# Odd input projection of a hybrid decoder trunk: VectorE's order inside a step (convolution taps and values, then the weight's low half, then the long taps)

## The chip, the cores and the metric

The kernel runs on one core of a Trainium2 chip. The metric is the device time of one execution in microseconds (us), median over runs; less is better. Engines are named as in the profile: PE is TensorE's matmul and PEld its weight load, DVE is VectorE, ACT is ScalarE, POOL is GpSimd, SP is the engine that issues most DMAs.

## The reference, cut to what matters

Two decoder layers over 512 tokens of width 1024. The change lies in layer 1 (the odd one), in its combined input projection and what is done to that projection's output while it is still being computed:

```python
p = h @ od_w_in[j]                       # 1024 -> 3600 columns
y_c = _conformer_conv(p[..., :o1], ...)  # val * sigmoid(gate), causal depthwise conv of 31 taps, LN, silu
y_d = _mamba2_ssd(p[..., o1:o2], p[..., o2:o3], p[..., o3:], ...)
# in _mamba2_ssd:
xbc = jax.nn.silu(_causal_dwconv(xbc, conv_w, conv_b))     # 4 taps over 1536 channels
dt = jax.nn.softplus(dt_raw + dt_bias)
xdt = x_c * dt_c[..., None]                                # the "values", per chunk of 128 tokens
states = jnp.einsum('bclgn,bclgh,bclghp->bcghpn', b_c, decay_to_end, xdt)
```

## The kernel before

All weights come as one stream of 512 KB chunks (128 x 1024 fp32), three slots deep (`W_SLOTS`). A product in fp32 accuracy is made of three fp32r products (`mm3`, lines 615 to 617), so each weight chunk is split first: ACT writes the high half (`w_hi`, line 1289), DVE subtracts it from the raw weights and writes the low half (`w_lo`, line 1822, `split`, which raises `w_split`). PE waits for `w_split` before a chunk. A chunk of the feature-major projection is 8 blocks of three 128x512 matmuls, 24 in all, into one of the 8 PSUM banks.

The odd input projection has 29 chunks: 0 to 7 are gates and values of the Conformer branch, 8 is dt, 9 to 20 are xbc 0 to 11, 21 to 28 are z. One loop of 29 steps on DVE and one on ACT run beside PE's 29 chunks, each engine in the written order. In step i:

- DVE splits chunk i+2 (`split(FIRST["in1"] + i + W_SLOTS)`), then does the 3 remaining taps of the short convolution of xbc i-10, which is chunk i-1 (`ssd_conv(i - 10)`, steps 10 to 21; it reads the PSUM bank, adds into `sconv`, and its third tap raises `xbc_out`), then some taps of the long convolution (`conf_taps`: 2 in each of steps 10 to 21, 4 in steps 22 and 23), then at a few steps small pieces (`conf_sum`, dt work in steps 9, 15, 16, 18), and in steps 20 to 23 the two multiplications `values(i - 20)` that empty the banks `sxt` into `xdt`.
- ACT makes `w_hi` of chunk i+2 (not before PE is through chunk i-1, whose slot it takes), waits for chunk i of PE, copies it with the first tap into `sconv` (`ssd_first(i - 9)`), makes three products for the long convolution (`conf_product`, tile `cprod`; the third waits for POOL's addition of the first), and applies the gate to the convolution of step i (`ssd_gate(i - 10)`, which waits for `xbc_out`).
- POOL adds the three products (line 584, `cacc2 <- cacc2 + cprod`), both operands in SBUF.
- PE computes chunk i. Between chunks it has inserted work: dt transposes before 15, `slast` before 18, `values_to_tokens(c)` (8 transposes into two `sxt` banks) before 20 + c, keys and scores before 24, chunk states before 25, and so on.

Banks go round in a fixed order worked out at build time (`TILES`, `BANK`, `AFTER`; `take` waits until the earlier tile of that bank is emptied). For the chunks that the prediction speaks of: chunk 15 takes the bank of xbc 3 (emptied in DVE's step 13), chunk 16 that of xbc 4 (step 14), chunk 17 that of xbc 5 (step 15), chunk 19 xbc 6 (step 16), chunk 20 xbc 8 (step 18), the `sxt` pair before 21 one of xbc 9 (step 19), chunk 21 xbc 10 (step 20), chunk 22 xbc 11 (step 21), chunk 23 the second `sxt` bank of `values(1)` (step 21), and chunk 24 the first `sxt` bank of `values(3)` (step 23). Chunk c also needs its low half, from step c-2.

Of the kernel before, what the change touches and what calls it, by code (L numbers as in the profile page):

```python
# [28 lines left out]
W_SLOTS = 3  # L29
# [35 lines left out]
FIRST = {}  # L65
# [105 lines left out]
def build(nc, x_tok, x_feat, mem_feat, weights, vectors, lora, lru_w, ln_rows, out):  # L171
    with ExitStack() as ctx:
# [177 lines left out]
        def xdt(c):  # L350

            return xdts[c // 2][:, c % 2]
# [13 lines left out]
        def S(name):  # L366
            if name not in sems:
                sems[name] = ctx.enter_context(nc.semaphore(name))
            return sems[name]

        def V(name, i):
            c = VEC[name] + i
            return vec[:, c:c + 1]

        def bank(stg, i):
            return ps[BANK[stg, i]]
# [6 lines left out]
        def made(kind, n):  # L383

            return S("mixer_mm"), MADE[kind][n - 1]
# [7 lines left out]
        def bc(ap, n):  # L393

            return ap.unsqueeze(2).to_broadcast([ap.shape[0], ap.shape[1], n])
# [1397 lines left out]
        def _(dve):  # L1793
# [3 lines left out]
            def step(ins, lag=0):  # L1797

                n_step[0] += 1
                ins.then_inc(S("dve_step"), 1)  # L1800
                if n_step[0] > lag:
                    dve.wait_ge(S("dve_step"), n_step[0] - lag)
# [3 lines left out]
            def done(ins, name):  # L1806

                counts[name] = counts.get(name, 0) + 1
                ins.then_inc(S(name), 1)
                dve.wait_ge(S(name), counts[name])  # L1810

            def f(ap):

                return ap.bitcast(F32)

            def split(upto):

                while n_split[0] < min(upto, N_CHUNKS):
                    c = n_split[0]
                    s = c % W_SLOTS  # L1820
                    dve.wait_ge(S("w_hi_done"), c + 1)
                    dve.tensor_tensor(w_lo[:, s], w_raw[:, s], f(w_hi[:, s]), ALU.subtract).then_inc(S("w_split"), 1)  # L1822
                    n_split[0] += 1
# [10 lines left out]
            def tt(o, a, b_, op):  # L1834
                return dve.tensor_tensor(o, a, b_, op)  # L1835

            def stt(o, a, s, b_, op0, op1):
                return dve.scalar_tensor_tensor(out=o, in0=a, scalar=s, in1=b_, op0=op0, op1=op1)  # L1838
# [277 lines left out]
            def scale_rows(n, t):  # L2116

                l, which = divmod(n, 3)
                dve.wait_ge(*of(f"lnt{l}_{which}", "_mm", 8))
                dve.wait_ge(S("gb_in"), 16 * (n + 1))  # L2120
                step(tt(h[:, t], h[:, t], gb[:, 0], MUL))

            def shift_rows(n, t):

                done(tt(h[:, t], h[:, t], gb[:, 1], ADD), "h_ready")
# [204 lines left out]
            def conf_taps(first, last):  # L2330

                for n in range(first, last):
                    j, k = divmod(n, DVE_TAPS)
                    k += POOL_TAPS + 1
                    at = CP - (CONF_TAPS - 1) + k
                    acc = bank("cacc", j)[:]
                    dve.wait_ge(S("c_first"), j + 1)
                    step(stt(acc, cu[:, j, at:at + T], V("ccw", 4 * k + j), acc, MUL, ADD))

            def conf_sum(j):  # L2340

                dve.wait_ge(S("c_add"), (POOL_TAPS - 1) * (j + 1))
                done(tt(cacc[:, j], bank("cacc", j)[:], cacc2[:, j % 2], ADD), "cacc_out")

            def ssd_conv(m):

                x_, d_ = bank("xbc", m), sconv[:, m % 2]
                dve.wait_ge(S("s_first"), m + 1)
                for k in range(1, 4):
                    ins = stt(d_[:, k:T], x_[:, 0:T - k], V("scw", 12 * (3 - k) + m), d_[:, k:T], MUL, ADD)  # L2350
                    if k < 3:
                        step(ins)
                    else:
                        done(ins, "xbc_out")

            def taps_by(i):

                at = [0, 0, 0, 3, 8, 13, 18, 23, 28, 31]
                return at[i] if i < 10 else min(31 + 2 * (i - 9) if i < 22 else 55 + 4 * (i - 21), 4 * DVE_TAPS)

            def by_head(ap):
                return ap.rearrange("p (h v) -> p h v", v=64)

            def values(c):

                for q in range(2):
                    dve.wait_ge(*made("sxt", 2 * c + q + 1))
                    done(tt(by_head(xdt(c)[:, q * HALF:q * HALF + HALF]), by_head(bank("sxt", 2 * c + q)[:]),
                            bc(stm[:, 0, c, 8 * q:8 * q + 8], 64), MUL), "sxt_out")

            def next_state(c):

                for g in range(2):
                    dve.wait_ge(*out_sem("sst", 2 * c - 2 + g + 1))
                    cols = slice(g * HALF, g * HALF + HALF)
                    nxt = by_head(prev[:, c, cols])
                    step(tt(nxt, by_head(prev[:, c - 1, cols]), bc(stm[:, 3, c, 8 * g:8 * g + 8], 64), MUL))
                    dve.wait_ge(*made("sst", 2 * c + g + 1))
                    done(tt(nxt, nxt, by_head(bank("sst", 2 * c + g)[:]), ADD), "sst_out")

            def grown(c):

                dve.wait_ge(S("h_moved"), 32)
                for g in range(2):
                    dve.wait_ge(*made("yoff", 2 * c - 2 + g + 1))
                    done(tt(by_head(yoff[:, c - 1, g * HALF:g * HALF + HALF]), by_head(bank("yoff", 2 * c - 2 + g)[:]),
                            bc(done_of(GROWTH, c)[:, 8 * g:8 * g + 8], 64), MUL), "yoff_out")
# [1 line left out]
            counts["sst_out"] = 2  # L2389
            step(dve.memset(cu[:, :, 0:CP], 0.0))  # L2390
            for i in range(29):
                split(FIRST["in1"] + i + W_SLOTS)
                if i < 4:
                    scale_rows(2, i)
                    shift_rows(2, i)
                if 2 <= i < 10 and i % 2 == 0:
                    j = i // 2 - 1
                    dve.wait_ge(S("cgate_out"), j + 1)
                    dve.wait_ge(S("chunk_done"), FIRST["in1"] + i)
                    done(tt(cu[:, j, CP:CP + T], bank("cval", j)[:], p1[:, 4 + j, PAD:PW], MUL), "cval_out")  # L2400
                if 10 <= i < 22:
                    ssd_conv(i - 10)
                if i:
                    conf_taps(taps_by(i - 1), taps_by(i))
                if i in (10, 14, 20, 24):
                    conf_sum((10, 14, 20, 24).index(i))
                if i == 9:

                    dve.wait_ge(S("s_sums"), 1)
                    dve.wait_ge(S("masks"), 2)  # L2410
                    raw = p1[0:16, DT, PAD:PW]
                    step(stt(sdt[:, 0], raw, 0.0, sdt[:, 0], ALU.max, ADD))
                    step(dve.tensor_scalar(raw, sdt[:, 0], small[0:16, 200:201], -1.0, MUL, MUL))
                    done(dve.tensor_tensor_scan(sdt[:, 1], m_scan[0:16], raw, 0.0, MUL, ADD), "s_acum")
                if i == 15:
                    for m in range(2):
                        dve.wait_ge(*made("stok", m + 1))
                        done(dve.tensor_copy(stm[:, m].rearrange("p c h -> p (c h)"), bank("stok", m)[:, 0:64]),
                             "stok_out")
                if i == 16:  # L2420
                    dve.wait_ge(S("masks"), 4)
                    dve.wait_ge(S("s_sums"), 2)
                    done(tt(to_sums[32:48], sdt[:, 1], f(sums_hi[:]), SUB), "s_alo")
                if i == 18:

                    dve.wait_ge(S("slast_out"), 1)
                    done(tt(stm[:, 2], stm[:, 3], stm[:, 1], SUB), "s_dte")
                if 20 <= i < 24:
                    values(i - 20)
                if i == 26:  # L2430
                    dve.wait_ge(*made("c", 1))
                    for j in range(4):
                        ins = stt(cacc[:, j], bank("cmean", 0)[:], -1.0 / 512, cacc[:, j], MUL, ADD)
                        done(ins, "c_cent")
                    done(dve.tensor_copy(small[:, 255:256], small[:, 254:255]), "cmean_out")
                    next_state(1)
                    grown(1)
                if i == 27:
                    next_state(2)
                if i == 28:  # L2440
                    grown(2)
# [163 lines left out]
```

## Time and profile before

| | us |
|---|---|
| median of 3 runs | 1705.49 |
| lowest and highest of the three | 1677.04, 1707.43 |
| the profiled execution | 1680.34 |
| its span | 1678.6 |

PE is busy 97% of the span, DVE 59%, ACT 44%, POOL 10%. The odd input projection takes the stretch from about 831 to 1031 us. A matmul's row is about 0.39 us long, but starts follow each other by 0.227 us (0.427 us at the half clock), since matmuls are pipelined: a chunk of 24 takes 5.44 us. In the rows below "idle before" in square brackets is the time for which the engine had nothing to do ahead of that instruction, and the arrow names who ended it. An xN at the end of a row means that N instructions were merged, in one duration.

### The profile page before, as it was taken

How to read it: one execution, taken by the hardware profiler on the slowest of the kernel's cores; microseconds unless marked ns; L12 is line 12 of the kernel's file. 1: busy time of each engine (PE TensorE's matmuls, PEld its weight loads, DVE VectorE, ACT ScalarE, POOL GpSimd, SP SyncE). 2: the span in 40 equal slices, each digit the busy share in tenths (PEclk: the TensorE clock that was granted, in tenths of full speed). 3: DMA queues.
4: the chain of work that ended last, by engine and by line, in shares of the span. 5: the costliest groups of instructions: out<-in, count | busy, mean ns of one | idle time of the engine just before them, and what ended most of it. 6: DMA issues, size and time to landing. Idle time of an engine off the chain costs nothing.

```text
span 1678.6 us, 24671 instructions
## 1 busy us (share of the span) xinstructions
PE 1620.1 (97%) x9954; PEld 1348.3 (80%) x9954; DVE 991.9 (59%) x1236; ACT 738.4 (44%) x987; POOL 168.9 (10%) x175
## 2 busy tenths in 40 slices
PE   7999999999999999999998899999999999999997
PEld 5777887988878888888786777879888788888886
DVE  3569767755676443434698955656656654444345
ACT  4545644555253232323457745634552532323232
POOL 5101201002000000000045620000020000000001
PEclk9999999999999999999999999999999999999999
DMA  5222004442223332334242220234411333323331
GB/s 201 68 88 64 16 4 151 140 149 63 84 81 101 100 101 88 101 96 130 63 149 78 88 73 4 101 128 149 139 64 56 108 102 100 100 89 102 99 125 63
DMA packets 41297, 159.60 MB, mean 95 GB/s; under 512 B 4576, under 2 KB 4704, under 8 KB 39776
## 3 DMA queue, kind: packets, MB, share of 16 engines
q1 hardware_dynamic: 40896, 155.93, 29.0%
q10 hardware_dynamic: 288, 2.10, 0.3%
q8 instruction: 79, 1.29, 0.3%
q14 instruction: 34, 0.28, 0.1%
HBM read 153.81 MB, written 4.19 MB: 94 GB/s over the span
## 4 chain that ended last, share of the span: by engine, by line
PE 83%; DVE 10%; ACT 4%; issue 1%; POOL 1%; DMA 0%; SPq 0%; DVEq 0%; ACTq 0%; POOLq 0%
PE bank L615 25%; PE bank L616 25%; PE bank L617 25%; DVE mix L1835 1%; DVE act_lo L1835 1%; DVE w_lo L1822 1%; PE bank L817 1%; PE bank L802 1%; DVE sconv L1838 1%; DVE h L1838 1%; DVE bank L1838 1%; PE bank L1138 1%; ACT w_hi L1289 1%; PE bank L1010 0%; DMA w_raw<-weights 0%
## 5 line engine op out<-in xcount | busy, mean ns | idle before, releaser
L1822 DVE TENSOR_TENSOR w_lo<-w_raw,w_hi 128x1024 fp32r<-128x1024 f32 x263 | 325.8, 1240 | 299.0 <-ACT w_hi L1289 295.9
L615 PE MATMUL bank<-act_lo,w_hi 128*128 128x512 f32 x1048 | 416.7, 398 | 28.8 <-DVE w_lo L1822 16.0
L1289 ACT ACTIVATE w_hi<-w_raw 128x1024 fp32r<-128x1024 f32 x263 | 278.9, 1061 | 348.9 <-PE bank L617 338.5
L616 PE MATMUL bank<-act_hi,w_lo 128*128 128x512 f32 x1048 | 411.4, 393 | 0.0
L617 PE MATMUL bank<-act_hi,w_hi 128*128 128x512 f32 x1048 | 411.0, 392 | 0.0
L615 PEld LDWEIGHTS bank<-act_lo,w_hi 128*128 128x128 f32 x1048 | 198.8, 190 | 78.3 <-issue 17.1
L617 PEld LDWEIGHTS bank<-act_hi,w_hi 128*128 128x128 f32 x1048 | 198.9, 190 | 42.2
L616 PEld LDWEIGHTS bank<-act_hi,w_lo 128*128 128x128 f32 x1048 | 198.8, 190 | 41.3 <-issue 1.2
L615 PE MATMUL bank<-w_lo,aux_hi 128*128 128x512 f32 x576 | 224.7, 390 | 0.0
L617 PE MATMUL bank<-w_hi,aux_hi 128*128 128x512 f32 x576 | 224.2, 389 | 0.0
L616 PE MATMUL bank<-w_hi,aux_lo 128*128 128x512 f32 x576 | 224.1, 389 | 0.0
L615 PEld LDWEIGHTS bank<-w_lo,aux_hi 128*128 128x128 f32 x576 | 108.1, 188 | 23.1 <-DVE w_lo L1822 0.7
L617 PEld LDWEIGHTS bank<-w_hi,aux_hi 128*128 128x128 f32 x576 | 108.1, 188 | 22.7
L616 PEld LDWEIGHTS bank<-w_hi,aux_lo 128*128 128x128 f32 x576 | 108.1, 188 | 22.0
L584 POOL TENSOR_TENSOR cacc<-cacc,cprod 128x512 f32<-128x512 f32 x52 | 71.9, 1382 | 484.7 <-ACT cprod L1631 482.2
L615 PE MATMUL bank<-w_lo,act_hi 128*128 128x512 f32 x288 | 113.5, 394 | 2.8 <-DVE w_lo L1822 2.3
L617 PE MATMUL bank<-w_hi,act_hi 128*128 128x512 f32 x288 | 112.9, 392 | 0.0
L616 PE MATMUL bank<-w_hi,act_lo 128*128 128x512 f32 x288 | 112.7, 391 | 0.0
L1835 DVE TENSOR_TENSOR stage<-stage 128x512 f32<-128x512 f32 x64 | 44.3, 692 | 105.7 <-ACT stage L1599 105.7
L1599 ACT ACTIVATE stage<-bank 128x512 f32<-128x512 f32 x64 | 38.2, 597 | 143.7 <-PE bank L617 143.7
L1835 DVE TENSOR_TENSOR aux_lo<-stage,aux_hi 128x512 fp32r<-128x512 f32 (+1 forms) x66 | 48.9, 741 | 61.7 <-ACT aux_hi L1601 53.6
L1601 ACT ACTIVATE aux_hi<-stage 128x512 fp32r<-128x512 f32 x64 | 40.5, 632 | 59.8 <-DVE stage L1835 59.8
(330 smaller groups left out, 1978.1 us busy)
## 6 DMA issues: line engine op xcount, KB each, us to landing
w_raw<-weights SPq DMA_DIRECT2D x263, 512.0 KB, 3.5
gb<-ln_rows SPq DMA_DIRECT2D x6, 1024.0 KB, 5.9
stage<-x_feat SPq DMA_DIRECT2D x4, 512.0 KB, 6.0
h<-x_tok SPq DMA_DIRECT2D x1, 2048.0 KB, 7.3
stage<-mem_feat ACTq DMA_DIRECT2D x2, 1024.0 KB, 6.4
spill<-h SPq DMA_DIRECT2D x1, 2048.0 KB, 6.9
h<-spill SPq DMA_DIRECT2D x1, 2048.0 KB, 7.9
out<-h SPq DMA_DIRECT2D x3, 512.0 KB, 2.6
```

The costliest lines, as they stand in the source:

```text
L584: pool.tensor_tensor(cacc2[:, j % 2], cacc2[:, j % 2], cprod[:, added % 2], ALU.add)\
L615: pe.matmul(o, whi, xlo, start=first, stop=False)
L616: pe.matmul(o, wlo, xhi, start=False, stop=False)
L617: return pe.matmul(o, whi, xhi, start=False, stop=last)
L802: last = each(lambda c, q, tok, feat, cf, ct: pe.matmul(compact(o, j, c, q, n), M_[b][tok, j, ct], halves(NBH[b][tok, j, ct], n, True), st ...
L817: last = each(lambda c, q, tok, feat, cf, ct: pe.matmul(compact(o, j, c, q, n), left[tok, j, ct], halves(right[tok, j, ct], n, v < 5), sta ...
L1289: act.activation(w_hi[:, s], w_raw[:, s], ACT.Copy).then_inc(S("w_hi_done"), 1)
L1599: done(act.activation(stage[:, n % 2], bank(f"up{l}_{q}", i)[:], ACT.Relu), "up_out")
L1601: done(act.activation(aux_hi[:, i], stage[:, 2 + n % 2], ACT.Copy), "up_hi")
L1822: dve.tensor_tensor(w_lo[:, s], w_raw[:, s], f(w_hi[:, s]), ALU.subtract).then_inc(S("w_split"), 1)
L1835: return dve.tensor_tensor(o, a, b_, op)
L1838: return dve.scalar_tensor_tensor(out=o, in0=a, scalar=s, in1=b_, op0=op0, op1=op1)
```

## The change

In steps 10 to 28 the split of chunk i+2 is moved behind the short convolution, and in steps 20 to 23 `values(i - 20)` is moved from behind the long taps and `conf_sum` to ahead of the split. Steps 0 to 9 are as they were. No instruction is added or removed, on any engine; no wait is added or removed. ACT's, PE's, POOL's and SP's programs are untouched.

```diff
             for i in range(29):
-                split(FIRST["in1"] + i + W_SLOTS)
+                if i < 10:
+                    split(FIRST["in1"] + i + W_SLOTS)
                 if i < 4:
                     scale_rows(2, i)
                     shift_rows(2, i)
...
                 if 10 <= i < 22:
                     ssd_conv(i - 10)
+                if 20 <= i < 24:
+                    values(i - 20)
+                if i >= 10:
+                    split(FIRST["in1"] + i + W_SLOTS)
                 if i:
                     conf_taps(taps_by(i - 1), taps_by(i))
...
-                if 20 <= i < 24:
-                    values(i - 20)
```

## Rows read from the trace of the kernel before

**Rows 1.** The page: busy time, share of the span and instructions of two engines.
```profile
PE 1620.1 (97%) x9954; PEld 1348.3 (80%) x9954; DVE 991.9 (59%) x1236; ACT 738.4 (44%) x987; POOL 168.9 (10%) x175
```

**Rows 2.** Who waited for whom, 884 to 1035 us: total us, times, longest us.
```profile
DVE w_lo L1822 <- ACT w_hi L1289: 35.8, 15, 8.4
POOL cacc L584 <- ACT cprod L1631: 38.1, 14, 7.7
...
PE bank L615 <- DVE sconv L1838: 5.7, 3, 4.0
PE bank L615 <- DVE w_lo L1822: 3.9, 2, 2.6
...
PE bank L615 <- DVE xdt L1835: 2.0, 1, 2.0
```

**Rows 3.** Timeline of PE: start us, us, engine, line, operation, names, [idle before <- releaser].
```profile
901.30 0.52 PE L615 MATMUL bank<-act_lo,w_hi 128*128 128x512 f32 x1 [2.56 <-DVE w_lo L1822]
...
921.57 0.50 PE L615 MATMUL bank<-act_lo,w_hi 128*128 128x512 f32 x1 [1.19 <-DVE sconv L1838]
933.24 0.50 PE L615 MATMUL bank<-act_lo,w_hi 128*128 128x512 f32 x1 [0.44 <-DVE sconv L1838]
961.40 0.80 PE L615 MATMUL bank<-act_lo,w_hi 128*128 128x512 f32 x1 [4.03 <-DVE sconv L1838]
...
969.35 0.93 PE L1059 MATMUL bank<-ident,p 128*128 128x128 f32 x7
...
975.70 1.03 PE L1059 MATMUL bank<-ident,p 128*128 128x128 f32 x8
...
986.86 0.78 PE L615 MATMUL bank<-act_lo,w_hi 128*128 128x512 f32 x1 [2.01 <-DVE xdt L1835]
994.04 1.88 PE L1088 MATMUL bank<-xdtd,bt 128*128 128x512 f32 x4
```

**Rows 4.** Busy time in four stretches: PE, PEld, DVE, ACT, POOL, granted clock, DMA, GB/s.
```profile
901.00:921.00 20.00, 19.07 (x80) 15.06 (x80) 17.17 (x23) 14.90 (x20) 11.49 (x11) 0.91 0.30 84
921.00:961.00 40.00, 35.36 (x162) 28.84 (x162) 36.93 (x48) 32.93 (x45) 26.02 (x21) 0.98 0.31 93
961.00:987.00 26.00, 23.58 (x113) 19.71 (x113) 20.81 (x28) 15.61 (x22) 7.94 (x6) 0.89 0.25 77
987.00:1033.00 46.00, 46.00 (x185) 33.27 (x185) 19.51 (x26) 16.51 (x23) 5.07 (x4) 0.96 0.11 35
```

**Rows 5.** Timeline of DVE: steps 10, 11, 15, 20, 22 and 23.
```profile
899.05 2.11 DVE L1822 TENSOR_TENSOR w_lo<-w_raw,w_hi 128x1024 fp32r<-128x1024 f32 x1
901.08 2.30 DVE L1838 SCALAR_TENSOR_TENSOR sconv<-bank,vec,sconv 128x511 f32<-128x511 f32 x3
...
906.58 1.23 DVE L1822 TENSOR_TENSOR w_lo<-w_raw,w_hi 128x1024 fp32r<-128x1024 f32 x1 [0.89 <-ACT w_hi L1289]
...
929.74 1.23 DVE L1822 TENSOR_TENSOR w_lo<-w_raw,w_hi 128x1024 fp32r<-128x1024 f32 x1 [0.50 <-ACT w_hi L1289]
930.88 2.31 DVE L1838 SCALAR_TENSOR_TENSOR sconv<-bank,vec,sconv 128x511 f32<-128x511 f32 x3
...
957.90 1.23 DVE L1822 TENSOR_TENSOR w_lo<-w_raw,w_hi 128x1024 fp32r<-128x1024 f32 x1 [0.34 <-ACT w_hi L1289]
959.04 2.31 DVE L1838 SCALAR_TENSOR_TENSOR sconv<-bank,vec,sconv 128x511 f32<-128x511 f32 x3
961.38 1.55 DVE L1838 SCALAR_TENSOR_TENSOR bank<-cu,vec,bank 128x512 f32<-128x512 f32 x2
...
977.87 1.42 DVE L1835 TENSOR_TENSOR xdt<-bank,stm 128x512 f32<-128x512 f32 x2
981.82 1.22 DVE L1822 TENSOR_TENSOR w_lo<-w_raw,w_hi 128x1024 fp32r<-128x1024 f32 x1 [2.53 <-ACT w_hi L1289]
982.96 3.12 DVE L1838 SCALAR_TENSOR_TENSOR bank<-cu,vec,bank 128x512 f32<-128x512 f32 x4
```

**Rows 6.** Timeline of ACT: its wait in iteration 10; high halves of chunks 20 to 22.
```profile
903.46 1.28 ACT L1662 ACT_TABLE_LOAD   x1 [2.57 <-DVE sconv L1838]
...
945.74 1.06 ACT L1289 ACTIVATE w_hi<-w_raw 128x1024 fp32r<-128x1024 f32 x1
...
951.17 1.07 ACT L1289 ACTIVATE w_hi<-w_raw 128x1024 fp32r<-128x1024 f32 x1
952.14 0.76 ACT L1645 ACTIVATE sconv<-bank,vec 128x512 f32<-128x512 f32 x1
...
956.74 1.06 ACT L1289 ACTIVATE w_hi<-w_raw 128x1024 fp32r<-128x1024 f32 x1
```

**Rows 7.** Timeline of POOL: additions beside a split, and later without one.
```profile
876.24 3.54 POOL L584 TENSOR_TENSOR cacc<-cacc,cprod 128x512 f32<-128x512 f32 x2 [0.37 <-ACT cprod L1631]
...
897.90 5.74 POOL L584 TENSOR_TENSOR cacc<-cacc,cprod 128x512 f32<-128x512 f32 x3 [0.41 <-ACT cprod L1631]
...
943.22 2.67 POOL L584 TENSOR_TENSOR cacc<-cacc,cprod 128x512 f32<-128x512 f32 x2 [2.53 <-ACT cprod L1631]
...
953.80 4.04 POOL L584 TENSOR_TENSOR cacc<-cacc,cprod 128x512 f32<-128x512 f32 x3 [1.40 <-ACT cprod L1631]
```

**Rows 8.** Timeline of DVE: the split that ran beside the first of Rows 7.
```profile
876.57 2.05 DVE L1822 TENSOR_TENSOR w_lo<-w_raw,w_hi 128x1024 fp32r<-128x1024 f32 x1
```

## Prediction, made before the change was run

> **What bounds the kernel now.** I read the page first. PE is busy 97% of the span [rows 1], so time can only be won where PE stands still or runs at the half clock. The change touches one loop, so the second view was who waited for whom in that loop. PE waits there for three writers on DVE: 5.7 us for the short convolution (sconv), 3.9 us for the split (w_lo) and 2.0 us for the values (xdt) [rows 2]. DVE itself waited 35.8 us for ACT's high half in the same stretch: it stands ahead of a split that isn't there yet, with other work behind it that could run.
>
> The third view, PE's timeline, gives each stop its place [rows 3]. By counting 5.44 us a chunk (24 x 0.227 us): 901.30 is the start of chunk 12, 921.57 of 15, 933.24 of 17, 961.40 of 21 and 986.86 of 24. The stops cost more than their idle time. Chunk 21 takes from 961.40 to 969.35, 7.95 us instead of 5.44, chunk 24 from 986.86 to 994.04, 7.18 us, and the granted clock is 0.91 and 0.89 in the two stretches that hold a long stop [rows 4]: after it the matmuls run for a while at 1.2 GHz instead of 2.4. So the stop ahead of 21 costs 4.03 + 2.5 = 6.5 us, that ahead of 24 2.01 + 1.7 = 3.7 us, those ahead of 15 and 17 1.2 and about 0.5 us without a slow stretch. About 12 us in all: that is the most the change can win back, since chunk 12's stop (2.56 us and some 1.7 at the half clock) is ended by a split that the change puts later.
>
> The pace of the others: ACT goes round in 951.17 - 945.74 = 5.43 and 956.74 - 951.17 = 5.57 us [rows 6], as long as a chunk. A full step of DVE is split 1.15 + convolution 2.34 + two taps 1.58 = 5.07 us from start to start [rows 5]. DVE has thus 0.4 us of slack per step and pieces of 0.5 to 0.9 us in six of the steps on top.
>
> **The change, part by part.** Nothing is added: DVE does the same 36 convolution taps, splits and values. Only order moves, and with it three things. Behind the moved split stand taps alone, and the convolutions now run in the time in which DVE waited for w_hi.
>
> *Step 10, a loss.* The split of chunk 12 ran at 899.05, and PE stood waiting for it [rows 3, 5]. Its w_hi was ready long before, so there is no wait to fill. Now the convolution's 2.30 us [rows 5] come first: it runs 899.05 to 901.4, the split from 901.4. Before it took 2.11 us, 0.88 more than the usual 1.23, because POOL was adding; POOL's three additions last until 903.6 [rows 7], so the split meets them again in part: it ends between 902.5 and 903.4 instead of 901.16. Chunk 12 starts 1.4 to 2.2 us later, and its longer stop may cost 0 to 0.8 us more at the half clock (by the difference between chunk 21's 2.5 and chunk 12's 1.7). I take +2.5.
>
> *Steps 13 and 15, a gain.* Chunk 15 waited for the convolution of step 13, 17 for that of step 15. In step 15 DVE stood 0.50 us for w_hi, split 1.15 us, and only then convolved [rows 5]. But PE needs the split of the same step as well (chunk 17 = 15 + 2), so it waits for the second of the two whichever is first. Only DVE's idle time is won, 0.34 to 1.06 us in seven of the steps 11 to 20 (0.89 in step 11, the first [rows 5]). The gate of ACT follows the convolution, so ACT comes to its next w_hi sooner: in iteration 10 it stood 2.57 us, until 903.46 [rows 6], for a convolution that now ends at 901.4. The delay of chunk 12 itself also gives DVE and ACT 2 us in which to catch up. With both, neither stop is left: -1.7 us.
>
> *Step 20, a gain.* Chunk 21 takes the bank of xbc 10, which is convolved in step 20, a chunk's time ahead and no more. Before, DVE ended step 19 at 957.56, waited 0.34, split 1.14, convolved until 961.35 [rows 5]. The split there is for chunk 22, which nobody needs yet. Moved behind, it gives 1.5 us at once: 959.9. What DVE has caught up by then comes on top. I chained the durations above from step 10 on, each start at the later of the engine's own last end and what it waits for, PE at 5.44 us a chunk with its insertions as before. With no split lengthened DVE's steps 11 to 20 start at 904.8, 909.9, 915.0, 920.0, 925.8, 931.4, 937.4, 942.4, 948.0 and 953.1 (5.07 us each, the small pieces, and 0.6 us of waits), and chunks 12, 15, 17 and 20 at 902.7, 922.4, 933.3 and 950.5. The convolution of step 20 ends at 955.4, before PE comes at 956.9: no stop at all, chunk 21 starts 4.5 us earlier and loses its slow stretch of 2.5.
>
> *Steps 20 to 23, a gain.* Values(3) came behind a wait of 2.53 us for w_hi, a split and four taps, at 986.1 [rows 5], though their transposes were through at 976.7 [rows 3]. Values(2) ended at 979.29; now values(3) come straight behind step 22, near 980 at the latest. PE is ready for chunk 24 at 986.86 - 2.01 = 984.85. The stop goes wholly: -3.7 us, in every case that I can make. The splits behind them have a whole chunk to spare (that of step 23 is for chunk 25).
>
> *Steps 24 to 28.* The split goes behind nothing new, as there is neither convolution nor values: 0.
>
> *What the moved splits meet, a loss.* A split reads two tensors in SBUF, as POOL's additions do. Where they overlapped, at 876.57, the split took 2.05 us instead of 1.23 [rows 8], and POOL's two additions 3.54 instead of 2.67 [rows 7]: 0.8 us lost on each side. In steps 11 to 20 of before no split met an addition, since each waited for w_hi, which ACT writes just as POOL's third addition ends. The convolution of 2.3 us put ahead pushes the split into the next round of additions unless DVE is early enough to wait for w_hi as before. It isn't in steps 10 to 13, by the chain. So at least four splits pay. If all pay 0.8 us, a step is 5.9 us against PE's 5.44, DVE never gets early, and the same chain gives stops of 0.4 to 0.8 us ahead of chunks 17, 18 and 19 and one of 3.5 us ahead of 21: step 20 starts at 960.5, and chunk 21 at 962.9.
>
> The Trainium skill (SBUF — State Buffer, on the port pair that VectorE and GpSimd share) says that a VectorE operation with two SBUF inputs and a GpSimd one lock each other out for a whole instruction, and the loser waits. By that rule one meeting would cost the split what is left of an addition, up to 1.3 us, and the sum would lie between the cases below; the rows at 876 us agree with it, 0.8 us for an addition that had begun 0.33 us earlier.
>
> **The sum**, taken where the stream of chunks stands at 21 (what was lost at 12 and won at 15 and 17 is in its start) and at 24. With no meeting: chunk 21 starts at 956.9 instead of 961.4, -4.5; its slow stretch goes, -2.5; chunk 24's stop goes, -3.7: -10.7 us. With 0.8 us in every step: +1.5 (962.9), 0, -3.7: -2 us. With half of that in every step, which for step 20 is the same as the first five paying in full and the others nothing: the chain puts chunk 21 at 960.0, -1.4, behind a stop of 2.7 us that leaves a slow stretch like chunk 12's (1.7 instead of 2.5), -0.8, and -3.7: -6 us. I take this, since the first four or five splits meet additions and later ones need not. Behind chunk 24 PE has no stop until 1037 and DVE is busy 19.51 of 46.00 us [rows 4], so all of it lasts to the end: every transfer, split and ACT step there follows PE.
>
> The profiled execution took 1680.34 us, 1.7 more than its span. It lies 25 us below the median 1705.49, near the lowest run; the runs spread over 30.4 us, five times what I forecast. Against the profiled time the sum gives 1674.3; applied to the median, 1699.5.
>
> **Rivals.**
> - *No meeting with POOL* (DVE early enough from step 12 on). For it: the splits of 11 to 20 of before met none, and the convolutions of the new order leave DVE waiting for w_hi again once it has caught up. Against: steps 10 to 13. -10.7 us: 1694.8.
> - *Every split meets POOL.* For it: 26.02 us of POOL work in 40.00 us [rows 4], so two thirds of all moments. -2 us: 1703.5.
> - *Slower.* One mechanism: the meetings also hold up POOL, whose first addition releases ACT's third product. ACT's round is 5.44 us with no slack. If each meeting costs ACT 0.8 us too, w_hi comes ever later, the split waits for it and chunks 13 to 20 wait for the split: (5.44 + 0.8 - 5.44) x 8 = 6.4 us, plus chunk 12's 2.5, less the 3.7 us of chunk 24: +5 us, 1710.5. It decides from about 0.2 us a round (0.2 x 8 + 2.5 is over 3.7). Against: only a meeting with the first of the three additions holds ACT, and the splits that come late meet the second or third.
> - *No change at all*: PE waits for both split and convolution, and each stop only changes its name. True for 15 and 17, not for 21 and 24, where the split is for a later chunk. 0 us: 1705.5.
>
> **How the numbers follow.** Forecast (-4 to -8): 0.45. No meeting (-8 to -11): 0.2. Every split meets (-3 to -1): 0.2. No change: 0.05. Slower by 1 to 6: 0.1. All five lie within 2% (34 us), which is about what a measurement of this kernel can tell from no change. The range must hold the spread of the runs too: the low end is the lowest run with the largest gain that still carries weight, 1677 - 9 = 1668; the high end the highest run, 1707, as the losing cases are as likely as a gain on it. A drawn median at the low end would pass -2% (1671.4) only with a gain over 5.6 us: 0.04; slower by over 2%: 0.01; within: 0.95.
>
> **What would show it.** PE's stop ahead of chunk 24 gone, xdt written before PE is through chunk 23. The stop ahead of chunk 12 longer, 4 to 5 us. The stop ahead of chunk 21 below 3 us. DVE's waits for w_hi in 899 to 960 us shorter and now between sconv and w_lo. w_lo rows over 1.8 us, at least three, in steps 10 to 14, with POOL rows over 4.4 us for three additions. It is wrong if the stop ahead of 21 stays at 4 us, if new stops on w_lo stand ahead of chunks 13 to 20, or if a stop appears behind chunk 24.

## The result, and the profile after

| | before | changed |
|---|---|---|
| median, us (runs) | 1680.45 (7) | 1669.14 (7) |
| lowest and highest | 1676.78, 1707.43 | 1667.53, 1702.36 |
| ratio of the times, 95% interval | | 0.9943 (0.9927 to 0.9959) |

The ratio is a gain of 9.6 us, between 6.9 and 12.3 (1680.45 times one less the ratio). Some executions of every kernel here are 24 to 33 us longer than the rest, two of the three of before that were shown at first among them (so its median moved from 1705.49 to 1680.45 with four more runs), and the ratios in this document leave them out.

The profile of the changed kernel that is read here, "the change" from now on, was taken when the same kernel was run a second time: an execution of 1669.68 us with a span of 1668.0, so that its times can be laid beside those of before.

PE's timeline in it, the rows that answer to [rows 3]:

```profile
892.61 0.47 PE L615 MATMUL bank<-act_lo,w_hi 128*128 128x512 f32 x1 [1.38 <-DVE w_lo L1822]
...
902.36 0.77 PE L615 MATMUL bank<-act_lo,w_hi 128*128 128x512 f32 x1 [4.06 <-DVE w_lo L1822]
...
921.52 0.67 PE L1043 MATMUL bank<-ident,sdt 16*128 16x16 f32 x8
922.12 0.50 PE L615 MATMUL bank<-act_lo,w_hi 128*128 128x512 f32 x1
...
957.12 0.50 PE L615 MATMUL bank<-act_lo,w_hi 128*128 128x512 f32 x1
...
962.72 1.03 PE L1059 MATMUL bank<-ident,p 128*128 128x128 f32 x8
964.36 0.50 PE L615 MATMUL bank<-act_lo,w_hi 128*128 128x512 f32 x1 [0.61 <-DVE sconv L1838]
...
984.40 1.88 PE L1088 MATMUL bank<-xdtd,bt 128*128 128x512 f32 x4
```

The stop ahead of chunk 12 has grown from 2.56 to 4.06 us. Those ahead of 15, 17, 21 and 24 are gone; chunk 15 is the row at 922.12, chunk 21 that at 957.12. A small one is new, 0.61 us ahead of chunk 22. Next, who waited for whom, 884 to 1026 us (the same work as in [rows 2]):

```profile
DVE w_lo L1822 <- ACT w_hi L1289: 25.3, 7, 5.9
...
ACT cprod L1631 <- POOL cacc L584: 12.5, 11, 1.9
...
PE bank L615 <- DVE w_lo L1822: 5.4, 2, 4.1
...
PE bank L615 <- DVE sconv L1838: 0.6, 1, 0.6
```

PE's waits for sconv fell from 5.7 to 0.6 us and those for xdt from 2.0 to none, and those for w_lo rose from 3.9 to 5.4. DVE's own waits for w_hi fell from 35.8 to 25.3 us. The clock in the windows of [rows 4]:

```profile
901.00:921.00 20.00, 18.64 (x71) 15.20 (x72) 19.33 (x24) 16.56 (x22) 14.15 (x12) 0.83 0.34 105
921.00:961.00 40.00, 39.99 (x190) 32.88 (x189) 38.15 (x48) 31.33 (x42) 27.45 (x19) 1.00 0.27 82
961.00:987.00 26.00, 25.39 (x129) 20.72 (x128) 21.10 (x27) 18.09 (x26) 10.57 (x8) 1.00 0.29 98
```

It is lower behind chunk 12 (0.83 for 0.91) and full behind where 21 and 24 stood (1.00 for 0.98, 1.00 for 0.89). PE is busy 39.99 of the 40 us in the middle one, where it was busy 35.36 before.

**Where the time went**, each place counted from chunk 11's start (893.03 before, 892.61 in the change), since both executions are alike up to there:

| from chunk 11's start to | before | change | difference |
|---|---|---|---|
| chunk 12 | 8.27 | 9.75 | +1.5 |
| dt transposes ahead of 15 | 26.69 | 28.91 | +2.2 |
| chunk 15 | 28.54 | 29.51 | +1.0 |
| chunk 21 | 68.37 | 64.51 | -3.9 |
| transposes ahead of 22 | 76.32 | 70.11 | -6.2 |
| chunk 22's stop (0.61, new) | | | -5.6 |
| chunk states ahead of 25 | 101.01 | 91.79 | -9.2 |

The loop is 9.2 us shorter in these two traces, and the whole 9.6 by the ratio. So the gain isn't given back behind the loop.

### The profile page after: what moved, and what is told of

It is laid out like the page before. It is cut to its first block, busy times and chain, and to the rows that moved or that the text cites. A ratio compares the mean times of both kernels' runs of the same rounds, so it can differ in the third digit from the quotient of the medians.

```text
span 1700.6 us, 24671 instructions
## 1 busy us (share of the span) xinstructions
PE 1647.2 (97%) x9954; PEld 1376.9 (81%) x9954; DVE 992.4 (58%) x1236; ACT 738.4 (43%) x987; POOL 173.1 (10%) x175
## 4 chain that ended last, share of the span: by engine, by line
PE 85%; DVE 9%; ACT 3%; issue 1%; DMA 1%; POOL 0%; SPq 0%; DVEq 0%; ACTq 0%; POOLq 0%
PE bank L615 25%; PE bank L617 25%; PE bank L616 24%; PE bank L817 2%; PE bank L802 2%; DVE mix L1835 1%; DVE act_lo L1835 1%; DMA w_raw<-weights 1%; DVE sconv L1838 1%; PE bank L1138 1%; DVE w_lo L1822 1%; DVE bank L1838 1%; DVE h L1838 1%; PE bank L832 0%; PE bank L1010 0%
## 5 line engine op out<-in xcount | busy, mean ns | idle before, releaser
L584 POOL TENSOR_TENSOR cacc<-cacc,cprod 128x512 f32<-128x512 f32 x52 | 77.2, 1484 | 475.7 <-ACT cprod L1631 473.2
L615 PEld LDWEIGHTS bank<-w_lo,act_hi 128*128 128x128 f32 x288 | 54.4, 189 | 15.7 <-DVE w_lo L1822 2.7
```

Source lines behind the costliest of these rows:

```text
L584: pool.tensor_tensor(cacc2[:, j % 2], cacc2[:, j % 2], cprod[:, added % 2], ALU.add)\
L615: pe.matmul(o, whi, xlo, start=first, stop=False)
```

## Experiments

For each kernel D is the distance in its trace from the start of ACT's copy of chunk 8, which no variant moves, to the first chunk-state matmul ahead of chunk 25. It is 113.22 us before (880.82 to 994.04) and 104.01 in the change (880.39 to 984.40). D comes from one trace and the ratio from several executions; where they differ, more of that below. The change was traced twice, in executions of 1702.36 and 1669.68 us, and D is 104.10 and 104.01. The trace of the early split on DVE is of an execution of 1709.04 us.

| kernel | D, us | against before | ratio of times (95%) |
|---|---|---|---|
| the change, second measurement | 104.01 | -9.2 | 0.9951 (0.9934 to 0.9969) |
| values alone | 108.38 | -4.8 | 0.9985 (0.9976 to 0.9995) |
| split alone | 107.96 | -5.3 | 0.9983 (0.9972 to 0.9994) |
| split moved from step 11 | 108.69 | -4.5 | 0.9990 (0.9979 to 1.0001) |
| from step 13 | 108.89 | -4.3 | 0.9977 (0.9966 to 0.9988) |
| from step 20 | 106.93 | -6.3 | 0.9973 (0.9962 to 0.9985) |
| early split on DVE | 112.16 | -1.1 | none |
| early split on DVE and ACT | 112.07 | -1.2 | 1.0002 (0.9989 to 1.0016) |
| change, POOL's additions small | 99.78 | -13.4 | 0.9928 (0.9909 to 0.9948) |
| before, POOL's additions small | 105.55 | -7.7 | 0.9972 (0.9959 to 0.9985) |
| ACT's high half early, order from 13 | 101.37 | -11.9 | 0.9946 (0.9931 to 0.9960) |
| ACT's high half early, order from 10 | 99.54 | -13.7 | 0.9930 (0.9916 to 0.9945) |

**The two parts of the change, each alone.** First only the values are moved, then only the split:

```diff
                 split(FIRST["in1"] + i + W_SLOTS)
...
                 if 10 <= i < 22:
                     ssd_conv(i - 10)
+                if 20 <= i < 24:
+                    values(i - 20)
...
-                if 20 <= i < 24:
-                    values(i - 20)
```

> One part alone: values(i - 20) moved behind the short convolution, the split left at the head of the step. Theory (what stands ahead of chunk 24 is only the long taps, the split and the wait for w_hi): the stop of 2.0 us and its slow stretch of 1.7 us go, all others stay: -3.7 us, ratio 0.9978. Rival (in step 23 the wait for w_hi stands ahead of values(3) whatever their place behind the split): the stop stays within 1 us of 2.0, ratio 0.999 to 1.000.

```diff
-                split(FIRST["in1"] + i + W_SLOTS)
+                if i < 10:
+                    split(FIRST["in1"] + i + W_SLOTS)
...
                 if 10 <= i < 22:
                     ssd_conv(i - 10)
+                if i >= 10:
+                    split(FIRST["in1"] + i + W_SLOTS)
```

> The other part alone: the split moved behind the short convolution, values(i - 20) left behind the long taps. Theory (the parts add up to the -9.6 us): stops ahead of 15, 17 and 21 go, chunk 12's grows, chunk 24's of about 2 us stays: -5.5 us, ratio 0.9967. Rival (the parts need each other: with PE earlier by 4 us at chunk 21 and values(3) no earlier, the stop ahead of 24 grows to 4 us and more): -2 to -3 us, ratio 0.9985.

With the values alone PE's timeline has no stop ahead of chunk 24 and keeps the one ahead of 21:

```profile
962.10 0.80 PE L615 MATMUL bank<-act_lo,w_hi 128*128 128x512 f32 x1 [4.02 <-DVE sconv L1838]
```

With the split alone it is the other way round; this is 21 and 24:

```profile
958.57 0.50 PE L615 MATMUL bank<-act_lo,w_hi 128*128 128x512 f32 x1 [0.23 <-DVE sconv L1838]
...
982.57 0.50 PE L615 MATMUL bank<-act_lo,w_hi 128*128 128x512 f32 x1 [2.02 <-DVE xdt L1835]
```

So each stop belongs to one edit, and by D they are nearly independent: 4.8 and 5.3 make 10.1 us, and the change has 9.2. About 1.0 us of the 4.8 isn't the stop ahead of 24: behind the stop ahead of 21, as long as in before (4.02 us), five matmuls ran at the half clock instead of ten. The rival of the split alone (a stop of 4 us and more ahead of 24) didn't come, the stop there is 2.02. The stop ahead of chunk 12 is 4.08 us with the split alone and 2.59 with the values alone, so the loss there is the split's as well.

**The same kernel again, and the new order without step 10.** After the first result my theory was that step 10 is a plain loss: left in the old order, chunk 12 keeps its 2.56 us and the rest of the gain stays.

> The change itself, once more, to have its trace from an execution that can be set beside the one of before, and a tighter interval. Theory: the gain is 9 to 10 us, all of it inside the odd input projection: the stop ahead of chunk 12 grows from 2.56 to about 4.1 us, those ahead of 15, 17 and 24 are gone, that ahead of 21 is under 0.5 us. Rival (part of the 9.6 us came from elsewhere, outside the loop): PE's distance from the start of chunk 11 to the last chunk-state matmul ahead of chunk 25 shrinks by less than 7 us.

```diff
-                if i < 10:
+                if i < 11:
                     split(FIRST["in1"] + i + W_SLOTS)
...
-                if i >= 10:
+                if i >= 11:
                     split(FIRST["in1"] + i + W_SLOTS)
```

> The change without its step 10: there the split of chunk 12 stays ahead of the convolution. Theory (step 10 is a plain loss of 1.5 us of stop and 1.3 us at the half clock): -2.8 us on top of the change, -12 us against before, ratio 0.993. Rival (the early convolution of step 10 is what frees ACT 3 us sooner and lets it catch up with PE; without it the stop ahead of 21 comes back to 1.5 us or more): about the same time as the change or slower, ratio 0.994 to 0.997.

It fell. Chunk 12's stop is 2.58 us, as it should be, but PE then stops ahead of 13, where the change has no stop, and the one ahead of 21 is back, as the rival had it (PE's timeline, chunks 12, 13 and 21):

```profile
903.38 0.47 PE L615 MATMUL bank<-act_lo,w_hi 128*128 128x512 f32 x1 [2.58 <-DVE w_lo L1822]
...
912.61 0.77 PE L615 MATMUL bank<-act_lo,w_hi 128*128 128x512 f32 x1 [3.53 <-DVE w_lo L1822]
...
964.29 0.50 PE L615 MATMUL bank<-act_lo,w_hi 128*128 128x512 f32 x1 [2.12 <-DVE sconv L1838]
```

DVE's timeline, steps 11 and 12, and POOL's beside it tell how:

```profile
907.81 2.31 DVE L1838 SCALAR_TENSOR_TENSOR sconv<-bank,vec,sconv 128x511 f32<-128x511 f32 x3
910.16 2.31 DVE L1822 TENSOR_TENSOR w_lo<-w_raw,w_hi 128x1024 fp32r<-128x1024 f32 x1
...
916.31 2.23 DVE L1822 TENSOR_TENSOR w_lo<-w_raw,w_hi 128x1024 fp32r<-128x1024 f32 x1
```

```profile
910.12 4.84 POOL L584 TENSOR_TENSOR cacc<-cacc,cprod 128x512 f32<-128x512 f32 x3 [4.37 <-ACT cprod L1631]
...
916.18 1.28 POOL L584 TENSOR_TENSOR cacc<-cacc,cprod 128x512 f32<-128x512 f32 x1 [1.22 <-ACT cprod L1631]
```

The convolution of step 10 is late, so the gate is late, so ACT's next w_hi and products are late, and with them the split, which starts 0.04 us behind a POOL addition and takes 2.31 us instead of 1.23. In the change step 10's convolution comes first and ACT waits for it only 0.55 us instead of 2.57 [rows 6] (ACT's timeline of the change):

```profile
901.03 1.28 ACT L1662 ACT_TABLE_LOAD   x1 [0.55 <-DVE sconv L1838]
```

The 1.5 us that chunk 12 loses there buys the 3.53 us ahead of chunk 13.

**The split of chunk 12 ahead of the dt work.** If chunk 12's stop is only the wait for a split that stands behind dt operations, the split can be put ahead of them, first on DVE alone, then with ACT's high half early too:

```diff
# DVE, step 9, ahead of the dt operations
+                    split(FIRST["in1"] + 10 + W_SLOTS)
```

> The changed kernel, and in step 9 the split of chunk 12 ahead of the three dt operations (3.8 us) instead of behind them and the convolution. Theory (chunk 12 stands 4.1 us for a split whose w_hi lies ready early, and runs 3.0 us longer at the half clock): both go, -6 to -7 us on top of the change, ratio to before 0.990. Rival (the dt operations come later and dt transposes ahead of chunk 15 or the gate of ACT wait for them): -3 us or less on top.

```diff
# DVE as above, and ACT:
                 if i == 8:
+                    split(FIRST["in1"] + 9 + W_SLOTS)
                     raw = p1[0:16, DT, PAD:PW]
```

> As early_split, and on ACT the high half of chunk 11 ahead of the dt functions (about 4.8 us with two table loads) instead of behind them. Theory: the stop of 1.4 us ahead of chunk 11 goes too, -8 us on top of the change, ratio to before 0.989. Rival (ACT's dt chain is what is late, and what depends on it moves by the 1 us that w_hi takes): no gain over early_split.

Both took the gain away (D 112.16 and 112.07; the second is 1.0002 of before in time). With both splits early chunk 12 waits 1.30 us, but chunk 13 9 us (timelines of PE, ACT and DVE of this kernel):

```profile
913.54 0.76 PE L615 MATMUL bank<-act_lo,w_hi 128*128 128x512 f32 x1 [8.98 <-DVE w_lo L1822]
```

```profile
906.47 1.28 ACT L1662 ACT_TABLE_LOAD   x1 [5.82 <-DVE sconv L1838]
907.77 0.63 ACT L1662 ACTIVATE p<-sconv 128x512 f32<-128x512 f32 x1
908.43 1.06 ACT L1289 ACTIVATE w_hi<-w_raw 128x1024 fp32r<-128x1024 f32 x1
```

```profile
904.08 2.32 DVE L1838 SCALAR_TENSOR_TENSOR sconv<-bank,vec,sconv 128x511 f32<-128x511 f32 x3
...
911.09 2.31 DVE L1822 TENSOR_TENSOR w_lo<-w_raw,w_hi 128x1024 fp32r<-128x1024 f32 x1
```

Read in order of time: the early split pushes the dt work back, the first convolution comes at 904.08 instead of 898.64, ACT stands 5.82 us for it ahead of the gate, and only behind the gate, at 908.43, makes the high half that the split for chunk 13 needs. Convolution, gate, high half, split: a ring over two engines, and chunk 13 waits for its last link.

**The new order from step 13 and from step 20.** If it is the entry that matters, a later entry should miss the ring.

```diff
-                if i < 10:
+                if i < 13:
...
-                if i >= 10:
+                if i >= 13:
```

> The change with its new order from step 13 on; steps 10 to 12 keep the split first. Theory (the first step in which the split goes behind the convolution makes PE wait a convolution's 2.3 us once, as long as DVE is late; in split_from_11 that stop stood ahead of chunk 13, 3.5 us with a slow stretch of 2.7): by step 13 the stops of chunks 11 and 12 have let DVE catch up, PE needs both split and convolution there, so no new stop; distance from the start of chunk 11 to the chunk-state matmuls ahead of chunk 25 90 to 93 us (before 101.0, the change 91.8). Rival (a late start of the new order leaves ACT 2 us later all along, and the stop ahead of 21 stays over 2 us): 95 us or more, as split_from_11's 96.5.

> The new order in steps 20 to 28 alone, values included: what the change does for chunks 21 and 24 without anything ahead. Theory: the stops ahead of 12, 15 and 17 are those of before, the stop ahead of 21 shrinks by the split and the wait for w_hi (1.5 us) from 4.0 to 2.5, that ahead of 24 goes with its slow stretch: 6 us less in the loop, distance 95 us. Rival (the stop ahead of 21 shrinks only with what DVE catches up in steps 10 to 19): it stays at 4 us, distance 96.2 as with the values alone.

From step 20 it came nearly as expected (the same edit with 20): chunks 12 and 15 keep the stops of before, 24 has none, and 21 has 1.78 us instead of 4.03. The 0.44 us ahead of 17 are gone as well: behind chunk 15's stop seven matmuls ran slow here, so PE came to 17 later. New are 1.12 us ahead of 22. From 13 the expectation was missed: from chunk 11's start to the chunk states it is 96.7 us, where 90 to 93 were expected and the rival said 95 or more, and D is 2 us longer than from step 20. PE's timeline, chunks 15 and 21:

```profile
923.37 0.77 PE L615 MATMUL bank<-act_lo,w_hi 128*128 128x512 f32 x1 [1.67 <-DVE w_lo L1822]
...
963.00 0.50 PE L615 MATMUL bank<-act_lo,w_hi 128*128 128x512 f32 x1 [3.08 <-DVE sconv L1838]
```

The split for chunk 15, its first behind a convolution, took 1.77 us, those of steps 18 and 19 took 2.12 and 1.83, and that of step 21 2.37, where in the change they take 1.23, 1.22, 1.22 and 1.47: entered here, the order falls more often into a phase in which a split starts just behind an addition of POOL. By D eleven, thirteen and twenty are all worse than ten, which I had held for the step that only costs.

**POOL taken out of the meetings.** The additions of POOL shrink to 64 of their 512 columns, so that the rest of that partial sum is left out and hardly any meeting is left; once on the change, once on before:

```diff
-  pool.tensor_tensor(cacc2[:, j % 2], cacc2[:, j % 2], cprod[:, added % 2], ALU.add)
+  pool.tensor_tensor(cacc2[:, j % 2, 0:64], cacc2[:, j % 2, 0:64], cprod[:, added % 2, 0:64], ALU.add)
```

> The changed kernel with POOL's 52 additions of the long convolution cut from 512 to 64 columns; the other 448 columns of that partial sum are left out. POOL is then hardly busy and no split can meet an addition. Theory (what the meetings cost falls on POOL and on small operations of DVE, not on PE's path): the time stays within 2 us of the changed kernel, ratio to before 0.993 to 0.995. Rival (the meetings hold DVE or ACT and PE waits for them): another 3 us or more are won, ratio 0.992 or less.

> The kernel before with the same 52 additions cut to 64 columns (448 columns of the partial sum left out). Nothing of DVE's order changes; ACT's third product no longer waits 0.77 us, so that ACT's round is 4.7 us instead of 5.4. Theory (DVE's late convolutions come from its waits for w_hi, and those from ACT's round being as long as PE's chunk): the waits of DVE in steps 11 to 20 go, the stop ahead of 21 shrinks from 4.0 us to below 2, about -4 to -7 us, ratio 0.996 to 0.9975. Rival (order on DVE alone decides): the stop ahead of 21 stays over 3 us, ratio 0.999 or more.

On the change D falls by another 4.2 us. Chunk 12's stop is 2.64 us instead of 4.06, and no matmul behind it runs at the half clock; chunk 11's falls from 1.38 to 0.28. So the theory that the meetings cost PE nothing fell by D (by time the two intervals overlap). On before D falls by 7.7 us, and the theory with which I had sent it, that ACT's round with POOL in it is what makes DVE wait for w_hi and so makes the stop ahead of 21, fell: in steps 11 to 20 DVE's waits for w_hi go down only from 4.10 us in 7 places to 2.84 in 6, and the stop stays (PE's timeline, chunks 21 and 24):

```profile
957.64 0.80 PE L615 MATMUL bank<-act_lo,w_hi 128*128 128x512 f32 x1 [3.64 <-DVE sconv L1838]
...
982.05 0.50 PE L615 MATMUL bank<-act_lo,w_hi 128*128 128x512 f32 x1 [2.02 <-DVE xdt L1835]
```

ACT's round didn't get shorter. What it no longer waits for POOL (0.77 us a round) it now waits for DVE's convolution, 0.71 to 1.12 us in eight rounds behind its first gate, as here (ACT's timeline of this kernel):

```profile
918.76 0.63 ACT L1662 ACTIVATE p<-sconv 128x512 f32<-128x512 f32 x1 [0.71 <-DVE sconv L1838]
```

So neither of the long stops that the change removes is POOL's doing; they are order alone. What POOL costs in before is mostly in the entry, at chunks 11 and 12: of the 7.7 us 4.1 are won by the start of chunk 15. Much of the rest is the clock: behind 21 and 24 six and no matmuls run slow, where in before ten and seven do.

**The ring cut at ACT.** The experiments say that w_hi must not stand behind the gate. This puts ACT's high half right behind the first tap of each xbc chunk, with DVE's new order from step 13 in one kernel and from step 10 in the other:

```diff
                 elif stg == "xbc":
                     ssd_first(n)
+                    split(FIRST["in1"] + i + 1 + W_SLOTS)
...
                 if i == 8:
+                    split(FIRST["in1"] + 9 + W_SLOTS)
                     raw = p1[0:16, DT, PAD:PW]
```

> A version meant to be faster than the change: DVE's new order from step 13 on, and on ACT each high half right behind the first tap of the same iteration (from iteration 9 on) and that of chunk 11 ahead of the dt functions, so that no split waits behind products, gates or the dt chain. Theory (w_hi behind the gate, the gate behind the convolution is the ring that made early_both stop 9 us ahead of chunk 13): stops ahead of 11, 12 and 13 under 0.5 us each, DVE the tightest engine with 5.07 us a step, a stop of about 2.3 us ahead of 21: distance 86 to 88 us, 4 to 5 us less than the change, ratio to before 0.991 to 0.992. Rival (ACT's earlier w_hi puts splits onto POOL's additions, DVE's steps grow past PE's 5.44 us): as the change or slower, 0.994 or more.

> The same order on ACT with DVE's new order from step 10 on, as in the change. Theory: chunk 12 waits for a convolution of 2.3 us, about 2.5 us of stop and perhaps a slow stretch, 3 us more than act_early: distance 89 to 91 us. Rival (the early convolutions release ACT's gates, and that is worth more than the stop): as act_early or less.

By D the second is the best kernel here that computes the whole: D 99.54, ratio 0.9930, against 0.9943 and 0.9951 of the change. D is 4.5 us below the change's; the intervals of the times overlap, so by time alone it isn't shown to be the faster one. Its timeline of PE has four short stops behind chunk 11, ahead of 12, 13, 21 and 22, and its window the full clock throughout:

```profile
898.02 0.47 PE L615 MATMUL bank<-act_lo,w_hi 128*128 128x512 f32 x1 [0.93 <-DVE w_lo L1823]
...
904.37 0.47 PE L615 MATMUL bank<-act_lo,w_hi 128*128 128x512 f32 x1 [0.67 <-DVE w_lo L1823]
...
952.75 0.50 PE L615 MATMUL bank<-act_lo,w_hi 128*128 128x512 f32 x1 [1.30 <-DVE sconv L1839]
...
960.31 0.50 PE L615 MATMUL bank<-act_lo,w_hi 128*128 128x512 f32 x1 [0.95 <-DVE sconv L1839]
```

```profile
901.00:987.00 86.00, 83.09 (x392) 67.41 (x392) 76.11 (x93) 66.68 (x91) 55.22 (x38) 1.00 0.28 86
```

With the order from 13 a stop of 2.22 us stands ahead of chunk 15. The split that ends it took 2.35 us, and the three before it 2.16, 1.80 and 1.58. From chunk 11's start to the chunk states it has 90.7 us, where 86 to 88 were expected; the order from 10 has 88.9, below the 89 to 91 of its theory, as its rival said.

**What stays open.** For the variants the ratio gives 0.4 to 3 us less than D. The values alone have 4.8 us in D and 2.5 in time (0.15% of 1680), the split alone 5.3 and 2.9: by time the two parts make 5.4 us, where the change has 8.2 in the measurement beside them. D is one execution of each kernel, and the stretches around it aren't alike. It starts between 880.4 and 882.9 us, though no edit but POOL's small additions touches anything ahead of it, and before starts early (880.82). With the values alone the stretch behind the loop, up to the end, is 2.1 us longer than in before, 643.1 us against 641.05. Why these stretches differ isn't known, and one trace for each kernel doesn't settle it. The order among variants whose ratios overlap goes by D alone.

## Why the prediction was right or wrong

**The time, wrong, by its base.** "Applied to the median, 1699.5" took a gain of 6 us from 1705.49, a median of three. With seven runs the median is 1680.45. The prediction saw that the profiled execution lay near the lowest run and 25 us below that median, and read it as spread. Of the 30.4 us between 1699.5 and the measured 1669.1 this base is 25.1; against the profiled time the sum gave 1674.3, and the other 5.2 us are in the sum. The profiled execution was the better base, since its clock in each window could be read. That 1669.1 lies inside 1668 to 1707 is no merit of the sum: the range was made that wide for the spread of the runs, and a median under 1671.4 had been given 0.04.

**Which of the cases.** The forecast was -6 us; what came is between 6.9 and 12.3, which is the size of the rival without meetings (-10.7, "-8 to -11", given 0.2). The working for it holds nearly row by row. Its chain put DVE's steps 11 to 14 at 904.8, 909.9, 915.0 and 920.0; in the change, moved by the 0.42 us by which it is early at chunk 11, they start at 904.85, 909.92, 914.98 and 920.05. It put chunk 21 at 956.9; the same way it started at 957.54. Against the forecast's terms of -1.4, -0.8 and -3.7 us the table above has -3.9 at chunk 21, -2.3 for its slow stretch and -3.6 at chunk 24, and +0.6 for the new stop ahead of 22.

**Step 10, right.** "I take +2.5": the stop grew by 1.50 us, inside "1.4 to 2.2", and 11 slow matmul starts (0.43 us apart) instead of 8 made 0.7 more: +2.2 by the table. But "a loss" was only half of it. Without it, as the kernel from step 11 shows, more is lost at 13.

**Steps 13 and 15, right.** "Neither stop is left": none is. Between the dt transposes and chunk 15 the change gained 1.2 us, the stop of 1.19.

**Step 20, the term mis-sized.** Taken was a stop of 2.7 us with a slow stretch behind it; there was no stop and none. With the slow stretch (7.95 us before, 5.60 now) that is the gain that the forecast left out. The convolution ended only just in time:

```profile
954.75 2.32 DVE L1838 SCALAR_TENSOR_TENSOR sconv<-bank,vec,sconv 128x511 f32<-128x511 f32 x3
957.10 1.42 DVE L1835 TENSOR_TENSOR xdt<-bank,stm 128x512 f32<-128x512 f32 x2
958.55 1.22 DVE L1822 TENSOR_TENSOR w_lo<-w_raw,w_hi 128x1024 fp32r<-128x1024 f32 x1
```

It was done at 957.07 and chunk 21 started at 957.12 (DVE's timeline of the change). By the chain it should have ended at 955.4, and moved by 0.42 it ended at 957.49, so DVE lost about 2 us on the way, of which two small operations below hold 1.6. Nothing was to spare, and that shows a chunk later. From this convolution to the next DVE takes 7.24 us (954.75 to 961.99, with the values and `conf_sum`), while PE takes 6.63 for chunk 21 and the transposes behind it (957.12 to 963.75). The difference is the 0.61 us ahead of chunk 22, which the prediction didn't have; 0.59 to 0.63 stand there in four of the other kernels too.

**Chunk 24, right.** "The stop goes wholly: -3.7 us": 3.6 by the table, and the kernel with the values alone shows that it is their place: the stop is gone there too, with the split as in before. `xdt` of values(3) is written from 974.50, 4 us before PE comes to chunk 24.

**"So at least four splits pay", the step that failed.** The meetings were there, as said. The splits didn't pay, though the prediction had set the sign itself (three w_lo rows over 1.8 us in steps 10 to 14; there is none): in 884 to 987 us of the change all but one of the moved ones took 1.22 or 1.23 us, and that one 1.47. Groups by line there, in the change and then in before (count | busy us, mean ns | idle before):

```profile
L584 POOL TENSOR_TENSOR cacc<-cacc,cprod 128x512 f32<-128x512 f32 x39 | 58.5, 1501 | 29.4 <-ACT cprod L1631 27.6
...
L1822 DVE TENSOR_TENSOR w_lo<-w_raw,w_hi 128x1024 fp32r<-128x1024 f32 x16 | 19.8, 1240 | 4.5 <-ACT w_hi L1289 3.9
```

```profile
L584 POOL TENSOR_TENSOR cacc<-cacc,cprod 128x512 f32<-128x512 f32 x39 | 52.8, 1354 | 40.0 <-ACT cprod L1631 38.1
...
L1822 DVE TENSOR_TENSOR w_lo<-w_raw,w_hi 128x1024 fp32r<-128x1024 f32 x15 | 19.3, 1287 | 12.1 <-ACT w_hi L1289 11.9
```

POOL paid 5.7 us, on the same 39 additions, and a split became cheaper on the mean. POOL's timeline in steps 19 and 20 of the change:

```profile
952.32 4.81 POOL L584 TENSOR_TENSOR cacc<-cacc,cprod 128x512 f32<-128x512 f32 x3 [1.39 <-ACT cprod L1631]
958.54 5.13 POOL L584 TENSOR_TENSOR cacc<-cacc,cprod 128x512 f32<-128x512 f32 x3 [1.41 <-ACT cprod L1631]
```

Three additions take 4.04 us alone [rows 7]. The split of step 19 started at 952.03, 0.29 us ahead of them, and took 1.22 us; they took 0.77 more. With POOL 0.04 us ahead, in the kernel from step 11, the split took 1.08 us more. The price falls on the one that comes second, and it was wrong to charge it to the split wherever the two met. The row from which the 0.8 us came [rows 8] is itself such a case, a split 0.33 us behind an addition. This agrees with the Trainium skill (SBUF — State Buffer, on the shared port pair), by which whichever of the two starts first has the pair for its whole instruction. The prediction cited that rule with the loser's price and didn't ask who would be the loser. It also had it that in steps 11 to 20 of before "each waited for w_hi": three of the ten (935.32, 941.27 and 952.52) didn't, and began 0.1 to 0.6 us behind POOL's last addition.

Who comes second is a matter of phase and not of the order as such: with the same order entered from step 11 five of the splits took 1.84 to 2.36 us. So it is in part luck that none of them lost much in the change. Where the two rows start 0.01 us apart they don't tell who was first: POOL paid at 958.54, and the split (2.37 us, from 971.90) in the kernel from step 13.

**The slower rival, wrong.** It had ACT's round lengthened by POOL from 0.2 us on. POOL's additions did get longer, and ACT waited 12.5 us for them in 884 to 987 us instead of 9.7, but PE waited for w_lo in no place behind chunk 12. A delay on POOL stayed mostly in POOL's idle time, which fell from 40.0 to 29.4 us. *No change at all* fell with the stops ahead of 21 and 24.

## What to carry to other kernels

Where an engine writes two things that another waits for, look at which is due first, and let the one that isn't due stand behind the one that is, so that its own wait is filled: that won 9 of about 12 us here. Before you price a stop by itself, follow the written order round through the other engine (convolution, gate, high half, split): in such a ring a stop that is removed at its entry comes back larger one chunk later, and the cut that worked by D is the one that takes the late link out of the ring. Take the base of a forecast from an execution whose clock you can read, and charge a contention to the side that starts second.

## What was not expected of the hardware

- Small operations of DVE pay the meeting with POOL as well: a 16x512 addition took 1.80 us in the change where before had 0.84, and a 128x64 one 1.12 where before had 0.51. With POOL's additions small they take 0.68 and 0.22, so each lost more than its own length. DVE's timeline of the change:

```profile
936.53 1.80 DVE L1835 TENSOR_TENSOR to_sums<-sdt,sums_hi 16x512 f32<-16x512 f32 x1
...
948.52 1.12 DVE L1835 TENSOR_TENSOR stm<-stm 128x64 f32<-128x64 f32 x1
```

- Stops of nearly the same length were followed by different slow stretches: 2.56 us ahead of chunk 12 by 8 slow matmuls in before, 2.58 by 7 where the new order starts at 13, 2.59 by none with the values alone; 4.0 us ahead of 21 by 10 in before and by 5 with the values alone; 1.2 us ahead of 15 by none in before and by 7 where the new order starts at 20. A slow stretch can't be priced to better than a microsecond from the stop's length.
